# Down weights of odd and even experts in two homes, and no accumulator: a mixture-of-experts layer on one core

## What is computed

```python
h2 = rmsnorm(x, g_norm2) * (1 + sc2) + sh2
logits = h2 @ w_router + b_router
top_val, top_idx = lax.top_k(logits, 4)
gates = softmax(top_val)
for e in range(32):                     # the tokens of expert e
    x_glu, x_lin = split(h2[tok] @ w_gu[e] + b_gu[e])
    x_glu, x_lin = minimum(x_glu, 7), clip(x_lin, -7, 7)
    act = x_glu * sigmoid(1.702 * x_glu) * (x_lin + 1)
    acc[tok] += (act @ w_down[e] + b_down[e]) * gate
x = x + ga2 * acc                       # ga2: one row for the prompt, one for the sample
```

## Time and profile before

| what | value |
|---|---|
| median of three runs | 1317.74 us |
| the profiled execution | 1317.04 us |
| its span, first to last instruction | 1315.3 us |
| mean granted clock of TensorE | 0.935 |
| busy: PE, PEld, DVE, ACT, POOL | 1137.4, 502.5, 382.6, 201.1, 46.2 us |
| moved by the 16 DMA engines | 454.87 MB, 346 GB/s over the span |
| gate/up loads | 256 of 1024 KB |
| down loads | 128 of 1024 KB |
| instruction fetch, q8 and q14 | 24 and 13 packets |

### The profile page before, as it was taken

The page is one execution under the profiler, slowest core; times in us unless marked ns, Lnnn a source line. Parts: engine busy times, 40 slices in busy tenths (PEclk is TensorE's granted clock), DMA queues, the critical chain, the costliest instruction groups (busy, mean ns, idle before and its releaser), DMA issues.

```text
span 1315.3 us, 20487 instructions
## 1 busy us (share of the span) xinstructions
PE 1137.4 (86%) x6676; PEld 502.5 (38%) x6677; DVE 382.6 (29%) x1044; ACT 201.1 (15%) x419; POOL 46.2 (4%) x28
## 2 busy tenths in 40 slices
PE   3899997885977879689999989999999999869994
PEld 0557663453322323234433443443333333224431
DVE  0333643434132222212232124123232222221233
ACT  1322332214101111010101101110111111101110
POOL 0241110002000000000000000000000000000000
PEclk9898997896989989898999989999999999889898
DMA  9943316830899999999999999999999999999991
GB/s 380 351 164 104 129 64 250 343 125 10 356 415 418 419 418 418 418 418 416 378 417 417 417 357 408 417 365 415 418 418 419 418 418 418 417 417 417 405 407 52
DMA packets 93297, 454.87 MB, mean 346 GB/s; under 512 B 9900, under 2 KB 14636, under 8 KB 57324
## 3 DMA queue, kind: packets, MB, share of 16 engines
q1 hardware_dynamic: 85392, 448.03, 84.5%
q10 hardware_dynamic: 7868, 6.34, 1.6%
HBM read 451.17 MB, written 3.17 MB: 345 GB/s over the span
## 4 chain that ended last, share of the span: by engine, by line
PE 64%; DMA 19%; SPq 5%; DVE 5%; issue 4%; ACT 2%; DVEq 0%; POOL 0%; ACTq 0%
PE psum L860 24%; PE psum L886 12%; DMA ring<-w_gu 11%; PE psum L560 6%; SPq L481 5%; DMA ring<-w_down 5%; PE psum L905 4%; PE psum L769 3%; PE psum L569 2%; DMA csb<-const 2%; PE psum L829 2%; PE psum L524 1%; PE psum L837 1%; DVE work L1591 1%; DVE work L1587 1%
## 5 line engine op out<-in xcount | busy, mean ns | idle before, releaser
L860 PE MATMUL psum<-ring,work 128*32 128x512 f32 (+2 forms) x2048 | 429.6, 617 | 29.8 <-DMA ring<-w_gu 29.1
L860 PEld LDWEIGHTS psum<-ring,work 128*32 128x32 f32 (+2 forms) x2048 | 132.4, 133 | 278.1 <-issue 204.9
L886 PE MATMUL psum<-ring,work 128*32 128x256 f32 (+2 forms) x1504 | 219.4, 480 | 12.7 <-DMA ring<-w_down 9.8
L1602 DVE TENSOR_TENSOR work<-psum,work 128x320 f32<-128x320 f32 x256 | 109.9, 484 | 223.6 <-PE psum L905 222.5
L962 ACT ACTIVATE work<-psum 128x256 f32<-128x256 f32 (+6 forms) x207 | 89.1, 445 | 361.0 <-PE psum L886 224.5
L886 PEld LDWEIGHTS psum<-ring,work 128*32 128x32 f32 (+2 forms) x1504 | 91.8, 130 | 125.0 <-issue 95.3
L1572 DVE TENSOR_SCALAR work<-csb 96x128 bf16<-96x128 f32 x64 | 15.4, 279 | 419.1 <-PE psum L860 418.1
L1221 ACT ACTIVATE work<-work 128x128 f32<-128x128 f32 (+2 forms) x64 | 25.2, 393 | 565.0 <-DVE work L1586 563.7
L560 PE MATMUL psum<-h,ring 128*128 128x320 f32 x320 | 92.6, 448 | 1.2 <-ACT h L1000 1.2
L905 PE MATMUL psum<-work 32*128 32x320 f32 (+2 forms) x512 | 81.5, 474 | 1.1 <-ACT work L962 1.0
L829 PE MATMUL psum<-work 128*32 128x256 bf16 (+4 forms) x846 | 68.0, 319 | 6.9 <-DVE work L1560 3.6
(11 more groups left out here) (212 smaller groups left out, 649.3 us busy)
## 6 DMA issues: line engine op xcount, KB each, us to landing
ring<-w_gu SPq DMA_DIRECT2D x256, 1024.0 KB, 18.7
ring<-w_down SPq DMA_DIRECT2D x128, 1024.0 KB, 18.6
ring<-w_ada SPq DMA_DIRECT2D x12, 2048.0 KB, 8.8
ring<-w_in SPq DMA_DIRECT2D x7, 2048.0 KB, 30.1
ring<-w_out SPq DMA_DIRECT2D x2, 2048.0 KB, 11.2
x<-xT ACTq DMA_DIRECT2D x1, 1280.0 KB, 26.3
yT<-h SPq DMA_DIRECT2D x4, 320.0 KB, 2.2
work<-b_exp ACTq DMA_DIRECT2D x3, 384.0 KB, 13.8
```

The lines of the kernel that those rows point to most:

```text
L860: last = mm(o, xg[:, kk, 0:m], cols(ring[:, kk, :]), start=False, stop=kk == KD - 1)
L886: last = mm(o, actT[:, kk, 0:m], ring[:, GU_UNITS + kk // 2, c1_:c1_ + n], start=False, stop=kk == 7)
L1602: tt_(t_, bank[SPREAD_BANKS[u]][:, 0:T], t_, ALU.add).then_inc(acc_ready, 1)
```

## The change

The down weights get a second home. Those of even experts stay in units 8 to 11 of `ring`; those of odd experts go to the first 8192 columns of `work` (`LATE`). SP loads down(1) behind the gate/up rows of expert 0 and ahead of down(0), behind three new waits: the mLSTM state is computed, and k/v and the convolution's rows are stored, since their buffers lie in those columns. In the loop, gate/up of expert e is then followed by down of expert e+1. The loop of each engine over the experts goes over pairs, so that each half names its home, and the program holds the body of an expert twice in it.

The tiles of the expert stage move up by 8192 columns in `work`. To make room, otok and wpick go into h, whose contents are no longer needed then, and `acc` goes. ACT waits for the state's store ahead of its first split copy. DVE's `add` now multiplies the PSUM bank by gate2 and adds it into the residual x itself, in two instructions for each block (256 columns of the prompt, 64 of the sample). POOL's memset and the 16 final operations go; SP stores x in four parts behind one semaphore that DVE's last memset counts. The reading of the largest count moves from behind the last expert to behind expert 0.

```diff
+LATE = DN_UNITS * UNIT
+PAIRS = NE // 2
...
-        take4, at4 = region(0)
+        take4, at4 = region(LATE)
...
-        otok = take4(D)
...
-        wpick = take4(3, CAP)
-        xtok = h[:].rearrange("p k t -> p (k t)")[:, 0:D]
-        acc = take4(8, T)
+        hflat = h[:].rearrange("p k t -> p (k t)")
+        xtok = hflat[:, 0:D]
+        otok = hflat[:, D:2 * D]
+        wpick = hflat[:, 2 * D:2 * D + 3 * CAP].rearrange("p (t n) -> p t n", t=3)
...
+        down_units = [ring[:, GU_UNITS:UNITS, :], work[:, 0:LATE].rearrange("p (j n) -> p j n", j=DN_UNITS)]
...
             start(0, 0, 0)
-            expert(0, 0, 0, True, False)
-            with eng.Fori(1, NE - 1) as e:
-                expert(e, e, 0, False, False)
-            expert(NE - 1, NE - 1, 0, False, True)
+            expert(0, 0, 0, 0, 1, True, False)
+            most = eng.value_load(cmaxi[0:1, 0:1], min_val=0, max_val=T)
+            with eng.Fori(1, PAIRS) as i:
+                expert(2 * i - 1, 2 * i - 1, 0, 1, i, False, False)
+                expert(2 * i, 2 * i, 0, 0, i + 1, False, False)
+            expert(NE - 1, NE - 1, 0, 1, PAIRS, False, True)
             finish(NE - 1, 0)
-            most = eng.value_load(cmaxi[0:1, 0:1], min_val=0, max_val=T)
...
+            def load_gu(e, turn):
+                for j in range(GU_UNITS):
+                    sp.wait_ge(gu_used, (turn - 1) * GU_UNITS + (j + 1))
+                    sp.dma_start(ring[:, j, :], gu_rows[e, :, j, :]).then_inc(gu_full[j], 16)
+
+            def load_dn(j, e, odd):
+                sp.dma_start(down_units[odd][:, j, :].rearrange("p (k n) -> p k n", k=2), dn_rows[e, :, j, :, :]).then_inc(dn_full[odd][j], 16)
+
+            def reload_dn(e, turn, odd):
+                for j in range(DN_UNITS):
+                    sp.wait_ge(dn_used, (turn - 2) * DN_UNITS + (j + 1))
+                    load_dn(j, e, odd)
...
+            sp.wait_ge(state_ps, MLH)
+            sp.wait_ge(sb_stored, 16 * 3)
+            sp.wait_ge(conv_stored, 16 * 2)
+            for j in range(DN_UNITS):
+                load_dn(j, 1, 1)
+            for j in range(DN_UNITS):
+                sp.wait_ge(*used_before(PRE + (GU_UNITS + j) // 2 - SLOTS))
+                load_dn(j, 0, 0)
+            with sp.Fori(1, PAIRS) as i:
+                load_gu(2 * i - 1, 2 * i - 1)
+                reload_dn(2 * i, 2 * i, 0)
+                load_gu(2 * i, 2 * i)
+                reload_dn(2 * i + 1, 2 * i + 1, 1)
+            load_gu(NE - 1, NE - 1)
...
             for c in range(4):
-                sp.wait_ge(y_ready, 4 * (c + 1))
-                sp.dma_start(yv[:, 2 * c:2 * c + 2, :], h[:, 2 * c:2 * c + 2, :]).then_inc(y_stored, 16)
+                if c == 0:
+                    sp.wait_ge(y_ready, 1)
+                sp.dma_start(yv[:, 2 * c:2 * c + 2, :], x[:, 2 * c:2 * c + 2, :]).then_inc(y_stored, 16)
...
-                        pe.wait_ge(unit_full[GU_UNITS + kk // 2], turn * 16 + 16)
+                        pe.wait_ge(dn_full[odd][kk // 2], times * 16)
...
-                        last = mm(o, actT[:, kk, 0:m], ring[:, GU_UNITS + kk // 2, c1_:c1_ + n], start=False, stop=kk == 7)
+                        last = mm(o, actT[:, kk, 0:m], down_units[odd][:, kk // 2, c1_:c1_ + n], start=False, stop=kk == 7)
...
+            act_.wait_ge(state_stored, 16 * 2)
             for i in range(4):
                 part_hi(i)
...
-                    t_ = acc[:, FEATURES[4 * i + u], :]
-                    tt_(t_, bank[SPREAD_BANKS[u]][:, 0:T], t_, ALU.add).then_inc(acc_ready, 1)
+                    f = FEATURES[4 * i + u]
+                    for cols, sq_ in SEQ:
+                        last = stt(x[:, f, cols], bank[SPREAD_BANKS[u]][:, cols], mod[:, 40 + f, sq_:sq_ + 1], x[:, f, cols], ALU.mult, ALU.add)
+                    last.then_inc(acc_ready, 1)
...
-            nc.vector.memset(cmax, 0.0).then_inc(acc_closed, 1)
-            v.wait_ge(acc_closed, 1)
-            for kk in range(KD):
-                for cols, sq_ in SEQ:
-                    stt(h[:, kk, cols], acc[:, kk, cols], mod[:, 40 + kk, sq_:sq_ + 1], x[:, kk, cols], ALU.mult, ALU.add).then_inc(y_ready, 1)
+            nc.vector.memset(cmax, 0.0).then_inc(y_ready, 1)
...
-            g.wait_ge(xo_ps, 8)
-            nc.gpsimd.memset(acc, 0.0).then_inc(acc_ready, 1)
```

More of the change, by code:

```diff
@@ L253, in build @@
         slot_full = [sem(f"slot_full{i}") for i in range(SLOTS)]
-        unit_full = [sem(f"unit_full{i}") for i in range(UNITS)]
+        gu_full = [sem(f"gu_full{i}") for i in range(GU_UNITS)]
+        dn_full = [[sem(f"dn_full{odd}_{i}") for i in range(DN_UNITS)] for odd in range(2)]
         v_chain, a_chain, g_chain = sem("v_chain"), sem("a_chain"), sem("g_chain")
@@ L386, in build @@
         SEQ = ((slice(0, TP), 0), (slice(TP, T), 1))
[L388 to L394, removed]
+        gu_rows = w_gu.rearrange("o e (k p) n -> (o e) p k n", p=P)
+        dn_rows = w_down.rearrange("o e (j k p) n -> (o e) p j k n", p=P, k=2)
         def used_before(n):
@@ L427, in passes @@
                     start(b * NE, 0, b)
[L428 to L431, removed]
+                    expert(b * NE, 0, b, 0, b * PAIRS + 1, True, False)
+                    with eng.Fori(1, PAIRS) as i:
+                        expert(b * NE + 2 * i - 1, 2 * i - 1, b, 1, b * PAIRS + i, False, False)
+                        expert(b * NE + 2 * i, 2 * i, b, 0, b * PAIRS + i + 1, False, False)
+                    expert(b * NE + (NE - 1), NE - 1, b, 1, b * PAIRS + PAIRS, False, True)
                     finish(b * NE + (NE - 1), b)
@@ L472, in _ @@
                     sp.dma_start(early[:, slot], src).then_inc(slot_full[slot], 16)
-            for j, (dst, src) in enumerate(expert_units(0)):
-                sp.wait_ge(*used_before(PRE + j // 2 - SLOTS))
[L476 to L484, removed]
+            def load_gu(e, turn):
[8 more added lines that the diff above has]
+                    load_dn(j, e, odd)
+            for j in range(GU_UNITS):
+                sp.wait_ge(*used_before(PRE + j // 2 - SLOTS))
+                sp.dma_start(ring[:, j, :], gu_rows[0, :, j, :]).then_inc(gu_full[j], 16)
+            sp.wait_ge(state_ps, MLH)
[12 more added lines that the diff above has]
+            load_gu(NE - 1, NE - 1)
             sp.wait_ge(cnt_ready, 1)
@@ L857, in gate_up @@
                 for kk in range(k0, k1):
-                    pe.wait_ge(unit_full[kk], turn * 16 + 16)
+                    pe.wait_ge(gu_full[kk], turn * 16 + 16)
                     for o, cols in up_blocks(groups):
@@ L870, in turn_act, with down @@
                 last.then_inc(atr_ps, 1)
-            def down(turn, groups):
+            def down(turn, groups, odd, times):
                 m = CAP // groups
@@ L909, in start @@
                 pe.wait_ge(pick_ready, turn * 3 + 3)
-                pe.wait_ge(acc_ready, turn * 8 + 1)
+                if not isinstance(b, int):
+                    pe.wait_ge(acc_ready, turn * 8)
                 by_size(pe, n, b, lambda groups: (gather(turn, groups), turn_x(turn, groups)))
@@ L917, in spread_out, with expert @@
                 by_size(pe, n, b, lambda groups: scatter(i, turn, groups))
-            def expert(turn, e, b, begins, ends):
+            def expert(turn, e, b, odd, times, begins, ends):
                 n = count(pe, e)
@@ L930, in expert @@
                 by_size(pe, n, b, lambda groups: gate_up(6, 8, turn, groups))
-                pe.wait_ge(acc_ready, turn * 8 + 1)
+                if not begins:
+                    pe.wait_ge(acc_ready, turn * 8)
                 if not ends:
@@ L937, in expert @@
                     by_size(pe, after, b, lambda groups: turn_x(turn + 1, groups))
-                by_size(pe, n, b, lambda groups: down(turn, groups))
+                by_size(pe, n, b, lambda groups: down(turn, groups, odd, times))
                 pe.wait_ge(wpick_ready, turn * 3 + 3)
@@ L1596, in add @@
             def add(i, turn):
[L1597 to L1598 removed]
+                if i == 0 and not (isinstance(turn, int) and turn == 0):
+                    v.wait_ge(acc_ready, turn * 8)
                 for u in range(4):
                     v.wait_ge(sc_ps, turn * 8 + (4 * i + u + 1))
[L1601 to L1602 removed]
+                    f = FEATURES[4 * i + u]
+                    for cols, sq_ in SEQ:
+                        last = stt(x[:, f, cols], bank[SPREAD_BANKS[u]][:, cols], mod[:, 40 + f, sq_:sq_ + 1], x[:, f, cols], ALU.mult, ALU.add)
+                    last.then_inc(acc_ready, 1)
             def start(turn, e, b):
```

20 lines of the change are left out of this document (10 added, 10 removed).

## The result

The kernel after took 1423.89 us, the median of four runs (1416.89 to 1428.22), against 1317.43 us for the kernel before beside it: a ratio of 1.0799, interval 1.0772 to 1.0825. It is slower, as forecast, but by 106 us and not by 24; the time lies far above the range. The profiled execution took 1422.36 us, with a span of 1420.5 us.

What follows compares the result with a forecast made beforehand. Bound: the weight queue up to the last large expert, with standstills behind large experts, then TensorE and the tail. 25.7 + 0.6 - 1.9 = +24.4 us gave 1341.4, 1342 as a median; range 1313 to 1350.

Steps and rivals of the forecast that it cites:

- The loop of two: TensorE's expert loop with two bodies: code fetched again each turn, +25.7 us; chance of the whole forecast 0.58.
- the sum of five small experts times 5.1 = 25.7 us: Expert stage: 5.1 us of fresh-code gaps in gather and down, at five small experts on the path; bounds 0 to 36.
- the 3.67 us at VectorE's jump: Gap at VectorE's jump behind the last expert, used as +3.7 us upper bound for VectorE's and ScalarE's doubled bodies.
- most of it is hidden: Queue-bound stretches of the expert stage: refetching costs nothing there, as a small expert has 10 us to spare.
- five places: Small experts ahead of the first, third (two) and last large experts, and one behind the last: 5.1 us each.
- the upper bound (7.3 us a turn): Refetch at the five small experts: the whole difference between fresh-code and kept-code turns, 7.3 us each, 36 in all.
- The fetch ahead: SP's down weights loaded one expert ahead: same bytes behind the same waits, so 0 us, bounds -10 and +1.
- The rival of 10 us: Bytes moved into the quiet stretch count and code does not: expert stage ends 10.0 us sooner, 1306.4; chance 0.08.
- The doubled loops of VectorE and ScalarE: Expert loops on these engines: doubled bodies are small, 0 us, with +3.7 us for the dearest turn.
- The adds: VectorE's scaled adds beside gate_up: four take 0.7 us more, on the path once, between two small experts, +0.6 us.
- The tail: Behind the last expert: adds +1.5, value_load gone -0.5, final operations gone -4.9, stores together +2.0; together -1.9 us.
- The last large expert: Sign in the expert stage: its start at about 1217 us if right, about 1186 us if early bytes pay.

Runs made afterwards that it cites:

- e5: The kernel after with TensorE's 32 experts written out one behind the other, no loop or jump back: 1341.55 us, ratio 1.0178.
- e1: The kernel after with one expert body per loop on every engine, only down written twice on TensorE behind an odd/even branch: 1320.26 us, ratio 1.0018.
- e8: The kernel after with one-body loops, two down homes and SP's load order of before (gate/up of e, then down of e): 1315.25 us, ratio 0.9985.
- e4: The kernel before with the doubled loop body on VectorE and ScalarE alone, TensorE keeping one body: 1317.9 us, ratio 0.9999.
- e2: The kernel before with scaled adds into the residual, no accumulator or final operations, and the four stores together: 1315.95 us, ratio 0.9982.
- e9: The kernel before with TensorE's steps from the second scatter ahead of gate/up rows 6 and 7 written twice behind a parity branch, 1881 instructions: ratio 1.0739.
- e10: The kernel before with TensorE's steps from gate/up rows 6 and 7 on written twice behind a parity branch, 1816 instructions in the loop: ratio 1.0052.

## Why the prediction was wrong

**The loop of two: right in kind, wrong in size.** Code was fetched again each turn, as forecast: 168 packets where about 150 were named. The step that failed is the sum of five small experts times 5.1 = 25.7 us, bounds 0 to 36, for which about 106 were measured. Two things in it were wrong: the price of a turn left out the jump, and most of it was taken to be hidden.

First, its price. 5.1 us were the gaps that fresh code leaves inside a body, and those came as forecast (2.81 us at L909). But a loop that isn't kept has a place that the kernel before never shows: the jump back to code that is gone. There TensorE stood 83.4 us where it stood 18.7; no row of before could give that, and the term had no place for it. The nearest row, the 3.67 us at VectorE's jump, stood in the sum for another engine. A bound for the unknown jump belonged on top of the 36, at each of the 14 jumps back.

Second, "most of it is hidden, since a small expert in the queue-bound stretches has 10 us to spare". The trace of before spoke against that much room: a delay of TensorE can hide where it would else wait for weights, and those waits were 38.9 us in the whole run (29.1 and 9.8). At gate/up of the 15 small experts they were 27.6 us, 1.8 each and not 10. The change added 64.7 us at the jumps, 39.0 in the gaps and 37.7 in slower matmuls, 141 us in all. The 38.9 were used up, no wait for weights was left, and from 594 us on the queue carried 357, 330 and 373 GB/s: TensorE had become the bound of the stage. So the price fell on nearly every turn and not at five places.

That e5, with gaps and without the jump, loses 23 us, near the term's 25.7, is luck. In its profiled run the four large experts begin at 585.99, 750.52, 852.90 and 1222.15 us, against 582.17, 736.70, 834.07 and 1196.34 before. So it loses 3.8 us ahead of the first, 10.0 up to the second, 5.0 up to the third, 7.0 up to the last and 1.4 behind it; the five places would give 5.1, 0, 10.2, 5.1 and 5.1.

The clock was in the upper bound (7.3 us a turn) but not in the 25.7. It is granted lower in each kernel that refetches by a jump (0.896 to 0.905 over the run, against 0.935), and lower behind the stops. That the stops cause it is how the rows lie (4.84 us behind the jump against 2.75), not shown by itself.

The Trainium skill (Runtime: NRT & Kernel Launch, Instruction fetch mechanics) warns that a taken branch stalls for a fetch when its target isn't in the current window of two pages. The prediction drew the store's size and its blocks from that section and not this sentence. Of the stall the trace bears it out (4.34 to 7.32 us a jump), of the window it doesn't: loops of up to 1816 instructions, some seven packets, jump back without a fetch. "Mostly hidden", as the same section of the Trainium skill has it for straight code, holds by halves here: +1.78% in e5. Its 2048 instructions for TensorE come near, but loops of 1881 and 2033 were fetched again; here the measurement decides.

**The fetch ahead at 0: right.** SP's first gate/up reload started 4 us earlier (327.52 us, 331.62 before), the wait for down weights went, and with the loop of one (e1) the time is not shorter. The rival of 10 us, 1306.4, is refuted, and e8, with the same homes and the old order, is no slower.

**The doubled loops of VectorE and ScalarE at 0: right** (e4, 0.9999). **The adds:** forecast +0.6, at one place. In e2 the gather waits for them five times, 4.6 us together, where before shows no such wait; what of that reaches the end was not separated, and adds and tail together gain 2.4 us in e2 (forecast 1.3). **The tail:** forecast -1.9. In after:

```profile
1407.62 4.76 DVE L1629 SCALAR_TENSOR_TENSOR x<-psum,tiny,x 128x256 f32<-128x256 f32 x16 [11.92 <-PE psum L928]
...
1414.93 0.06 DVE L1660 MEMSET tiny<- 128x1 f32 x1 [2.55 <-issue]
1415.02 2.50 SPq L517 DMA_DIRECT2D yT<-x  x4
```

The adds grew by 1.49 us (forecast +1.5) against the earlier trace rows; the gap ahead of the memset shrank from 5.24 to 2.55 and not by 0.5; the four stores took 2.50 us in place of 3.92. From the first add to the end it is 12.9 us where it was 16.1: -3.2.

**The last large expert** was forecast at about 1217 us and began at 1298.19; that one row would have told the size of the miss.

## What to carry to other kernels

Before a loop's body is written twice, count its instructions on the engine that runs the most of them, and compare with what the trace shows to be kept; here, by the count above, a loop of 1816 on TensorE was kept and one of 1881 cost 7%, so what differs between two halves belongs behind a small branch (e1) and not in a second body. Where a change puts an engine in a state that the trace of before never shows, such as a jump to code that is gone, give it a bound for every turn of the loop and set the sum against the waits that the engine really has in the trace; "hidden behind the queue" holds only until those are used up. Moving bytes earlier in a full, ordered queue gains nothing if as many bytes still stand ahead of the load that the end waits for.

## What the runs showed that was not expected

- The step lies between 1816 and 1881 instructions of TensorE by the count above, at 7.1 to 7.4 packets of 254. Why there is open: the loop's begin may lie inside a packet, or packets fetched ahead past the loop's end may push out its first. This was not tried.
- Once a loop misses, the time hardly depends on by how much: 77, 115 and 127 packets in the stage went with ratios of 1.0739, 1.0775 and 1.0799. With the least miss (e9) it is nine stops of 5.71 to 8.99 us, where after has thirteen of 4.34 to 7.32.
- Without the jump, 141 packets in the run (e5) cost 1.8%; with it, 112 (e9) cost 7.4%.
- A jump to code that is gone stands 4.3 to 7.3 us beside a full weight stream and 1.7 to 5.0 with thin loads, 49.8 us in the run in place of 83.4. Why so much remains with the queues nearly empty stays open.
- A branch onto code that was never fetched stood 10.0 us once (e1, L922), and 7.6 us once in e10.
